# Attention scores of the first block from three float32r products instead of one float32 product, with the gate rows spilled to make room

## What is computed

```python
q = (rms_norm(c_q, q_norm) @ w_q_up).reshape(b, s, 8, 96)        # rank 256 -> 8 x 96
kv = (rms_norm(c_kv, kv_norm) @ w_kv_up).reshape(b, s, 8, 128)   # rank 128 -> keys 64, values 64
q = concat([q_nope, apply_rope(q_rope)]); k = concat([k_nope, apply_rope(k_rope)])
scores = einsum("bqhd,bkhd->bhqk", q, k) * 96 ** -0.5
mask = key_chunk <= q_chunk                                       # chunks of 64 tokens
probs = softmax(where(mask, scores, -inf)); o = probs @ v
```

## Time and profile before

| | us |
|---|---|
| median of 3 runs (2779.86 to 2781.82) | 2780.64 |
| the profiled execution, its own time | 2778.42 |
| its span in the profile | 2776.6 |
| attention of the first block, from the first maximum to the last values' products | 282 to 467 |
| delta rule after it | from 467 |

### The profile page before, as it was taken

One profiled execution on the slowest core, in us unless ns is written; L12 is line 12 of the kernel. 1 busy time (PEld: TensorE's weight loads), 2 busy tenths in 40 slices (PEclk: granted clock), 3 DMA queues, 4 the chain that ended last, 5 costly groups with the idle time before them and its releaser, 6 DMA issues.

```text
span 2776.6 us, 39285 instructions
## 1 busy us (share of the span) xinstructions
PE 2643.3 (95%) x15530; PEld 2137.2 (77%) x15530; DVE 1879.3 (68%) x2265; ACT 1237.7 (45%) x2316; POOL 408.6 (15%) x354
## 2 busy tenths in 40 slices
PE   7999998999799999999999999899998999999997
PEld 6887566887688888888778888655677888888886
DVE  3466554664687777888974664489646655578889
ACT  3323565332777773333553333467316433343332
POOL 4322001347300000000300000001375000000002
PEclk9999999999999999999999999999999999999999
DMA  3210000004356664332323123411253232343333
GB/s 135 54 38 15 8 6 25 3 21 171 106 168 211 189 198 164 117 121 107 137 91 121 62 91 106 168 60 35 89 196 112 101 111 103 122 164 109 121 106 122
DMA packets 213489, 290.49 MB, mean 105 GB/s; under 512 B 16552, under 2 KB 143807, under 8 KB 213311
## 3 DMA queue, kind: packets, MB, share of 16 engines
q1 hardware_dynamic: 195918, 227.75, 24.8%
q10 hardware_dynamic: 17392, 60.30, 5.5%
HBM read 220.91 MB, written 67.11 MB: 104 GB/s over the span
## 4 chain that ended last, share of the span: by engine, by line
PE 78%; DVE 11%; ACT 4%; POOL 3%; issue 3%; DMA 1%; SPq 0%; ACTq 0%; DVEq 0%; POOLq 0%
PE ps L1739 7%; PE ps L1741 7%; PE ps L1740 7%; PE ps L1794 6%; PE ps L1796 6%; PE ps L1795 6%; PE ps L1877 4%; PE ps L1879 4%; PE ps L1878 4%; PE ps L1530 3%; PE ps L1436 2%; PE ps L1309 1%; PE ps L1311 1%; PE ps L1310 1%; PE ps L1676 1%
## 5 line engine op out<-in xcount | busy, mean ns | idle before, releaser
L1794 PE MATMUL ps<-down_t_hi,down_s_hi 128*128 128x512 f32 x896 | 349.4, 390 | 4.0 <-DVE acc L3332 2.2
L1796 PE MATMUL ps<-down_t_hi,down_s_lo 128*128 128x512 f32 x896 | 348.7, 389 | 0.0
L1795 PE MATMUL ps<-down_t_lo,down_s_hi 128*128 128x512 f32 x896 | 348.6, 389 | 0.0
L2492 ACT CAST down_s_hi<-down_a 128x2048 fp32r<-128x2048 f32 x56 | 107.2, 1915 | 368.7 <-PE ps L1796 327.1
L1142 POOL TENSOR_SCALAR mean_sq<-ssq 128x1 f32<-128x1 f32 x64 | 36.6, 571 | 1294.7 <-ACT squares_junk_ffn L2030 1244.6
L1739 PE MATMUL ps<-act_hi,up_hi 128*128 128x512 f32 (+1 forms) x544 | 205.7, 378 | 6.1 <-issue 2.8
L1740 PE MATMUL ps<-act_lo,up_hi 128*128 128x512 f32 (+1 forms) x544 | 204.9, 377 | 0.0
L1741 PE MATMUL ps<-act_hi,up_lo 128*128 128x512 f32 (+1 forms) x544 | 204.8, 376 | 0.0
L1794 PEld LDWEIGHTS ps<-down_t_hi,down_s_hi 128*128 128x128 f32 x896 | 168.2, 188 | 41.7 <-issue 7.4
L1796 PEld LDWEIGHTS ps<-down_t_hi,down_s_lo 128*128 128x128 f32 x896 | 168.2, 188 | 35.3
L1795 PEld LDWEIGHTS ps<-down_t_lo,down_s_hi 128*128 128x128 f32 x896 | 168.2, 188 | 34.6
(11 more groups left out here) (383 smaller groups left out, 6511.6 us busy)
## 6 DMA issues: line engine op xcount, KB each, us to landing
down_a<-hid_spill SPq DMA_DIRECT2D x32, 1024.0 KB, 6.6
hid_spill<-up_hid ACTq DMA_DIRECT2D x30, 1024.0 KB, 6.2
w_ada<-in_w_ada SPq DMA_DIRECT2D x48, 512.0 KB, 4.0
up_raw<-in_w_in SPq DMA_DIRECT2D x18, 1024.0 KB, 5.1
raw<-in_w_out SPq DMA_DIRECT2D x32, 512.0 KB, 3.7
up_raw<-in_w_up SPq DMA_DIRECT2D x16, 1024.0 KB, 5.6
down_b<-in_w_down SPq DMA_DIRECT2D x16, 1024.0 KB, 6.5
up_raw<-in_w_mlp_in SPq DMA_DIRECT2D x16, 1024.0 KB, 5.3
```

The costliest lines, as they stand in the source:

```text
L1794: pe.matmul(out, ops["s_hi"][:, k, cols], ops["t_hi"][:, k, :], start=first, stop=False, skip_group_check=True)
L1795: pe.matmul(out, ops["s_hi"][:, k, cols], ops["t_lo"][:, k, :], start=False, stop=False, skip_group_check=True)
L1796: mm = pe.matmul(out, ops["s_lo"][:, k, cols], ops["t_hi"][:, k, :], start=False, stop=last, skip_group_check=True)
```

## The change

- The query and key tiles become two sets each, `q_hi`, `k_hi`, `q_lo`, `k_lo`. A score product becomes three float32r products. A width under 256 columns is made 256.
- High parts are written by ACT (`mla_take` into the hi tiles; `mla_rope_high` for the rotated rows), low parts by DVE from PSUM (`mla_low_part`) and from `rope_t` (`mla_rope_low`). Rotation sums go into `rope_t` instead of the query tile.
- The low tiles lie where the gate rows lay: SP stores the gate rows to memory (`gate_out`, eight transfers of 256 KB) after the panel loads, and brings them back (`gate_back`) when the last pair's scores have begun. `key_rotation` waits for the store, `gdn_out` for the return.
- For the first pair the projections come in the order 0, 2, 4, 1, 3, 5 (first halves first). `mla_rotate(0, 1)`, the last panel's silu, the low part of chunk 5 and the scales move from before the attention into steps 0, 1, 2, 3 and 10 of the first pair on DVE. PE's projections of the next pair wait for DVE's low parts where they waited for ACT's copies.
- The out-norm multiply of the gate rows moves behind all eight gated products.

```diff
+MLA_FIRST = (0, 2, 4, 1, 3, 5)
+MLA_FIRST_BANKS = (7, 1, 0, 3, 2, 6)
+MLA_FIRST_FEATS = (2, 5, 2, 5, 3, 6)
...
+        q_lo = [[sb(f"q_feat_lo{x}{h}", kb, [P, SEQ], F32R) for h, kb in enumerate(kbs)] for x, kbs in enumerate(((169, 173), (65, 69)))]
+        k_lo = [[sb(f"k_feat_lo{x}{h}", kb, [P, SEQ], F32R) for h, kb in enumerate(kbs)] for x, kbs in enumerate(((177, 181), (49, 53)))]
...
+            for t in range(NT):
+                sp.wait_ge(sem("gate_silu"), NT + t + 1)
+                sp.dma_start(gate_d[t], gate[:, t, :]).then_inc(sem("gate_out"), 16)
...
+            sp.wait_ge(sem("mla_scores"), SB_ITEMS * (MLA_PAIRS - 1))
+            for t in range(NT):
+                sp.dma_start(gate[:, t, :], gate_d[t]).then_inc(sem("gate_back"), 16)
...
-                if i and n in (2, 3):
-                    pe.wait_ge(sem("proj_read"), 8 * i + 2 * n - 1)
+                if i == 1 and n == 0:
+                    pe.wait_ge(sem("mla_feat_done"), MLA_FEAT_AT[0, "low", 1])
+                elif i == 1 and n == 1:
+                    pe.wait_ge(sem("mla_feat_done"), MLA_FEAT_AT[0, "sum", 1])
+                elif i and n in (2, 3):
+                    pe.wait_ge(sem("mla_feat_done"), MLA_FEAT_AT[i, "low", n - 2])
...
-                    pe.wait_ge(sem("proj_read"), 8 * i + 7)
+                    pe.wait_ge(sem("mla_feat_done"), MLA_FEAT_AT[i, "low", 4])
...
-                    w = min(HALF, n - f * HALF)
-                    mm = pe.matmul(ps[:, 2 * h + f, 0:w], q_f[i % 2][h][0:DQK, t * P:(t + 1) * P],
-                                   k_f[i % 2][h][0:DQK, f * HALF:f * HALF + w], start=True, stop=True)
+                    w = max(min(HALF, n - f * HALF), 2 * P)
+                    q, k = slice(t * P, (t + 1) * P), slice(f * HALF, f * HALF + w)
+                    pe.matmul(ps[:, 2 * h + f, 0:w], q_hi[i % 2][h][0:DQK, q], k_hi[i % 2][h][0:DQK, k], start=True, stop=False)
+                    pe.matmul(ps[:, 2 * h + f, 0:w], q_hi[i % 2][h][0:DQK, q], k_lo[i % 2][h][0:DQK, k], start=False, stop=False)
+                    mm = pe.matmul(ps[:, 2 * h + f, 0:w], q_lo[i % 2][h][0:DQK, q], k_hi[i % 2][h][0:DQK, k], start=False, stop=True)
...
             def mla_pair(i):   # ACT
...
+                    if i == 0 and s == 2:
+                        mla_rope_high(0, 1)
+                    if s in (5, 7) and not last:
+                        mla_rope_high(i + 1, s // 2 - 2)
+                    if i == 0 and s == 10:
+                        mla_key_copy(0, k_hi, k_hi[0][0])
+                        mla_key_copy(1, k_hi, k_hi[0][0])
+                    if i == 0 and s == 12:
+                        mla_key_copy(0, k_lo, k_lo[0][0])
+                        mla_key_copy(1, k_lo, k_lo[0][0])
...
+            def mla_low_part(i, n):   # DVE
+                cols = slice(n % 2 * HALF, (n % 2 + 1) * HALF)
+                hi, lo = (q_hi, q_lo) if n < 2 else (k_hi, k_lo)
+                dve.wait_ge(sem("proj_read"), mla_took(i, n))
+                for h in range(2):
+                    ins = dve.tensor_tensor(lo[i % 2][h][0:NOPE, cols], ps[h * NOPE:(h + 1) * NOPE, MLA_BANKS[n] if i else MLA_FIRST_BANKS[n], :],
+                                            hi[i % 2][h][0:NOPE, cols].bitcast(F32), ALU.subtract)
...
             def mla_pair(i):   # DVE
...
-                    if i == 0 and s == 5:
-                        dve.wait_ge(sem("v_prod"), NT)
-                        dve.tensor_copy(k_f[1][1][rr, :], k_f[0][0][rr, :]).then_inc(sem("mla_k_rope_done"), 1)
+                    if i == 0 and s == 0:
+                        mla_rotate(0, 1)
+                    if i == 0 and s == 1:
+                        conv_silu(GDN_PANELS - 1)
+                    if i == 0 and s == 2:
+                        mla_low_part(0, 5)
+                    if i == 0 and s == 3:
+                        mla_rope_low(0, 1)
+                    if i == 0 and s == 10:
+                        gdn_scales()
...
-                    if s - 1 in MLA_STEPS[2:4] and not last:
-                        mla_rotate(i + 1, MLA_STEPS.index(s - 1) - 2)
+                    if s in (2, 3) and not last:
+                        mla_low_part(i + 1, s - 2)
+                    if s == 4 and not last:
+                        mla_rotate(i + 1, 0)
+                    if s == 5 and not last:
+                        mla_rope_low(i + 1, 0)
+                    if s == 6 and not last:
+                        mla_rotate(i + 1, 1)
+                        mla_low_part(i + 1, 4)
+                    if s == 7 and not last:
+                        mla_rope_low(i + 1, 1)
+                    if s == 9 and not last:
+                        mla_low_part(i + 1, 5)
+
+            mla_rotate(0, 0)
+            mla_low_part(0, 0)
+            mla_low_part(0, 4)
+            key_low()
+            mla_rope_low(0, 0)
+            mla_low_part(0, 1)
             mla_max(0, 0)
```

More of the change, by code:

```diff
@@ L1492, in mla_pair @@
                         mla_sums(i, 0)
-            for n in range(MLA_CHUNKS):
+            for n in MLA_FIRST:
                 pe.wait_ge(sem("lat_feat_done"), MLA_FIRST_FEATS[n])
@@ L1500, in _ @@
             for t, b in enumerate(V_BANKS):
-                name, count = (("mla_k_rope_done", 1), ("mla_k_rope_done", 1), ("proj_read", 3), ("proj_read", 5),
-                               ("mla_rope_done", 1), ("mla_rope_done", 2), ("proj_read", 7), ("proj_read", 9))[t]
+                name, count = (("mla_k_rope_done", 1), ("mla_k_rope_done", 1), ("mla_feat_done", MLA_FEAT_AT[0, "low", 0]),
+                               ("mla_feat_done", MLA_FEAT_AT[0, "sum", 0]), ("mla_feat_done", MLA_FEAT_AT[0, "low", 4]),
+                               ("v_done", 1), ("v_done", 2), ("v_done", 3))[t]
                 pe.wait_ge(sem(name), count)
@@ L2106, in _, with mla_rope_high, mla_key_high, mla_key_copy @@
                 .then_inc(sem("g_exp_done"), 1)
+            rr = slice(NOPE, DQK)
+            def mla_rope_high(i, n):
+                cols = slice(n * HALF, (n + 1) * HALF)
+                act.wait_ge(sem("mla_feat_done"), MLA_FEAT_AT[i, "sum", n])
+                for h in range(2):
+                    act.copy(q_hi[i % 2][h][rr, cols], rope_t[rr, h * HALF:(h + 1) * HALF]).then_inc(sem("rope_hi"), 1)
+            def mla_key_high():
+                act.wait_ge(sem("mla_k_rope_done"), 1)
+                for h in range(2):
+                    act.copy(k_hi[0][h][rr, :], k_sum[rr, :]).then_inc(sem("rope_hi"), 1)
+            def mla_key_copy(h, dst, src):
+                act.copy(dst[1][h][rr, :], src[rr, :].bitcast(F32)).then_inc(sem("rope_hi"), 1)
+            def mla_take(i, n):
+                cols = slice(n % 2 * HALF, (n % 2 + 1) * HALF)
+                act.wait_ge(sem("mla_proj"), mla_chunk_count(i, n))
+                for h in range(2):
+                    act.copy((q_hi if n < 2 else k_hi)[i % 2][h][0:NOPE, cols],
+                             ps[h * NOPE:(h + 1) * NOPE, MLA_BANKS[n] if i else MLA_FIRST_BANKS[n], :]).then_inc(sem("proj_read"), 1)
             def conv_panel(i, j):
@@ L2201, in mla_pair @@
                         mla_out(i, 0)
[L2203 to L2204 removed]
+            mla_take(0, 4)
+            mla_key_high()
+            mla_take(0, 1)
+            mla_rope_high(0, 0)
+            mla_take(0, 5)
             for t, b in enumerate(V_BANKS):
@@ new lines, in mla_rope_low @@
+            def mla_rope_low(i, n):
+                cols = slice(n * HALF, (n + 1) * HALF)
+                dve.wait_ge(sem("rope_hi"), FROM["rope_hi"] + mla_rope_hi(i, n))
+                for h in range(2):
+                    ins = dve.tensor_tensor(q_lo[i % 2][h][rr, cols], rope_t[rr, h * HALF:(h + 1) * HALF],
+                                            q_hi[i % 2][h][rr, cols].bitcast(F32), ALU.subtract)
+                ins.then_inc(sem("mla_feat_done"), 1)
+                dve.wait_ge(sem("mla_feat_done"), MLA_FEAT_AT[i, "rope_low", n])
```

137 lines of the change are left out of this document (79 added, 58 removed).

## The result

| | before | changed |
|---|---|---|
| median of five runs, us | 2780.64 (2779.29 to 2781.93) | 2795.67 (2793.36 to 2796.73) |
| ratio to the kernel before, 95% interval | | 1.0052 (1.0037 to 1.0067) |
| profiled execution: own time, span, us | 2778.4, 2776.6 | 2793.4, 2791.6 |
| mean granted clock | 0.985 | 0.984 |

The changed kernel is 15.0 us slower, twice what was forecast (+7.7 us by the sum, named as 2788.0); it lies inside the range 2775 to 2798 and in the direction with the largest chance, but just outside the +2 to +14 that the prediction called the forecast's own range.

What follows compares the result with a forecast made beforehand. PE was taken as nearly full in the first block's attention, with DVE close to the path in pairs' first halves. Terms +6.5 + 3.2 - 2.0 = +7.7 us on 2778.4 gave 2786.1, named 2788 as median; range 2775 to 2798.

Steps and rivals of the forecast that it cites:

- pair 3: Last pair of the first block's attention: prepares no next pair, gets only PE's saving of 2.3, counted as -2.0 us.
- The scores on PE: Score products in the attention: three float32r products instead of float32 save 9.3 us of PE time, 2.3 in each pair.
- Ahead of pair 0: Stretch before the first pair: DVE work leaves and low parts come, so maximum 0 is 0.6 us earlier.
- Pair 0: First pair of the attention: DVE becomes the bound in steps 0 to 9; +6.5 us, bounds +3 to +10.
- the walk itself: Queue-by-queue timing of pair 0's first steps, putting maximum 10 at 312.3 instead of 305.1, 7.2 us later.
- Pairs 1 and 2: Middle pairs: PE waits some 3 us for low part 4; +1.6 us each, bounds for one -2 to +4.
- Rival (b): PE's new holes in pairs 0 to 2 lower its clock, adding 3 to 5 us: 2792; chance 20%.
- (a): DVE's additions in steps 2 to 9 of pairs 0 to 2 are hidden, PE's saving passes: 2771; chance 10%.
- (c): The sides cancel: pair 0 costs 4 us, pairs 1 and 2 nothing, +2 in all: 2782.6; chance 18%.
- (d): Three score products cost what two float32 records cost, so PE saves nothing: +14.7 us, 2795; chance 2%.
- At nothing: Gate rows' store and way back, and their multiplies moved behind eight products, outside the attention's path: no cost.
- What would show it: Expected trace signs: DVE without holes in pair 0, maximum 10 later by 7 and 3 us, score waits some 55.

Runs made afterwards that it cites:

- e3: Changed kernel with one float32 score product on the high tiles instead of three float32r products, low parts still made but left out of the result: 2803.4 us.
- e5: e1 with the second rotation of pairs 1 to 3 put back to its old step, after the maximum of step 6: 2778.4 us.
- e2: Changed kernel with DVE's low part of chunk 4 before the second rotation instead of behind it: 2791.9 us.
- e4: Changed kernel with spare products, results overwritten, keeping PE busy while it waits for DVE's low parts: 2789.0 us.
- e6: Changed kernel with pair 0's second rotation, two low parts, last panel's silu and block scales put back ahead of the first maximum: 2802.2 us.
- e10: Kernel before with only the gate rows' spill, return and second-pass multiply added: 2780.9 us, ratio 1.0001.
- e1: Changed kernel with DVE's low parts one column wide and all three score products reading the high tiles: 2778.9 us.
- e11: e9 with the rotated rows projected first for pairs 1 to 3: 2772.7 us, 0.9970 of the kernel before.
- e9: Changed kernel's three products for pairs 1 to 3 with high and low parts made on GpSimd, pair 0 as in the kernel before: 2782.1 us.
- e12: Kernel before, float32 scores and nothing spilled, with the rotated rows projected first: 2778.6 us.

## Why the prediction was right, and by how much it was off

The direction, the place and the mechanism of DVE's queue were right; the size was half of what was measured, and a second mechanism, the clock, was left out of the sum. DVE's additions to the first halves cost more than PE's cheaper scores give back; pair 0 is worst; pair 3 gains; the rest of the program is untouched. Point by point:

- **The scores on PE, -9.3 in all.** The term is too large. In the second halves of pairs 1 and 2 the saving was 0.94 us (16.98 to 16.04), not 1.4; pair 3 gave -1.7, not -2.0, and four times that is 6.7. e3's 7.7 holds some clock too. Start to start, the first float32r product behind a turn takes 0.31 to 0.32 us (303.15 to 303.46) where the earlier trace rows gave 0.23 between products in a row. (The 0.47 in the expectation of e5 is such a record's duration.)
- **Ahead of pair 0, 0.6 earlier.** It was 0.4 later, 1.0 off, inside the bounds named there (1 earlier to 2 later). This point moves with the clock ahead of it: e2, which has the changed kernel's work up to there, began pair 0 3.0 us earlier.
- **Pair 0, +6.5: the step that failed.** It measured +10.5, above its upper bound of +10. The forecast had maximum 10 at 312.3 and 0.7 less to the pair's end. It came at 316.0, and the end added 0.2 more. By e4, where PE does not wait at half clock there, maximum 10 is at 314.4. So 1.6 of the 3.7 us is clock; 1.0 is the later start; the other 1.1 is the walk itself, or the half clock behind the hole at 292.88, which e4 did not take away (0.91 from 282 to 300). The second half lost PE's saving: 17.2 us against 17.0, where 0.7 less was forecast. The trace has ACT's key copies ahead of what PE waits for there; e6 rules the scales out. That the key copies alone do it was not tested.
- **Pairs 1 and 2, +1.6 each.** They cost 3.2. In e4 they are 49.36 us, +1.65: the queue's part was sized right, with two errors that cancel (the first halves +2.6 instead of +3.0, the second -0.9 instead of -1.4). The other 1.5 us of each is the half clock behind the hole of 3.77 us, which the prediction foresaw as "some 3 us" but at full clock.
- **Rival (b), the clock, 20%.** It was put as an alternative to the forecast, with 2792. It came together with it, in all three pairs, at 4.7 us by rows and 6.7 by medians: its own 3 to 5 for what it took. The objection to it was that holes of up to 2 us had left the clock at 1.00. That was one execution: in e10 the same hole of 1.93 us halved the clock. Of the earlier trace rows, which the prediction calls on for a long idle gap of PE, only 470 to 480 has idle time; from 220 to 230 the clock fell with PE busy for 10.00 of 10 us. With PE kept busy the kernel is at 2789.0 by its median, beside the forecast's 2788 (by its trace, whose last maximum is at 465.3, it is still 11.0 us above the kernel before, against 7.7). This is the error of method: a rival that follows from the forecast's own holes should have been a term of its sum.
- **Rivals (a), (c), (d).** (a) would need the additions hidden; e1 says they and their effects are 16.8 us. (c) fell with pair 0's +10.5 and the +3.2 of pairs 1 and 2. (d) named 2795, the number nearest to what was measured, and it is refuted by e3, by pair 3's -1.7 and by the products 0.23 apart: there the number would have been right by luck.
- **At nothing.** e10 has the spill, its way back and the multiplies in a second pass at 1.0001. That moving work into pair 0 gives back 4.4 to 6.5 us (e6) was not foreseen as a gain; the prediction had costed this part as 6.9 us more of work in pair 0 against 0.6 earlier ahead of it, without asking what the old place would cost once low parts are added.
- **What would show it.** As named: no hole of DVE between maxima 1 and 10 of pair 0 (the largest is 0.51 us up to maximum 8; then 1.71 and 1.99 for PE at half clock), three records 0.23 apart, a hole ahead of each last projection. Maximum 10 came 10.7 us later in pair 0, not 7, and 4.1 in pair 1 counted from its start, not 3. Waits for scores fell to 63, not to 55.

What stays open: how the 1.1 us of pair 0's walk divide, why the medians give the half clock 6.7 us and the traces 4.7, and by which condition a hole of 1.9 us halves the clock or doesn't. Not tried was e11 with GpSimd's key rows made after pair 0's rotations.

## What to carry to other kernels

A cheaper product needs its operands made, and the price is paid by whoever makes them, at the moment when others queue behind: here some 7 us less of PE brought DVE's low parts on the path, which cost 17 us with the clock behind them, while an idle engine could do the same work (e9) and leave the time as it was. Once a bound has moved, a hole of TensorE can have a second price behind it, its clock, 1.5 us for each of these; count it in the sum, not beside it. And a saving on the bound engine passes only as far as its waits allow: 0.7 us of 2.3 with the rotations beside GpSimd's work, 2.1 once they were moved.

## What the runs showed of the hardware that was not expected

Beside GpSimd's operations, one form of DVE's operations keeps its length and another one doubles. In e11 GpSimd makes a high and a low part of key rows while DVE works on a rotation; the two timelines:

```profile
285.23 1.04 POOL L1244 TENSOR_SCALAR k_feat_hi<-k_feat 32x1024 fp32r<-32x1024 f32 x1
286.35 2.33 POOL L1247 TENSOR_TENSOR k_feat_lo<-k_feat,k_feat_hi 32x1024 fp32r<-32x1024 f32 x1
```

```profile
285.63 0.69 DVE L2957 TENSOR_TENSOR rope_tmp<-ps,rope_trig 64x512 f32<-64x512 f32 x1
286.33 0.68 DVE L2958 TENSOR_TENSOR rope_tmp<-ps,rope_trig 64x512 f32<-64x512 f32 x1
287.05 2.88 DVE L2961 TENSOR_TENSOR q_feat<-rope_tmp 32x512 f32<-32x512 f32 x2
...
292.22 1.38 DVE L2961 TENSOR_TENSOR q_feat<-rope_tmp 32x512 f32<-32x512 f32 x2
```

DVE's products with one operand in PSUM take their usual 0.69 and 0.68 us beside GpSimd, the first one begun while GpSimd's operation ran. The sums, whose operands both lie in SBUF, take 2.88 instead of 1.38: they end 1.25 us after GpSimd's operation does, at 289.93 against 288.68. The Trainium skill (SBUF — State Buffer, on the two separate sides of SBUF) has a rule for this: DVE operations with two SBUF inputs and GpSimd's share a pair of ports, and whoever comes second is blocked until the other's instruction ends. The trace agrees: 1.63 us of overlap (287.05 to 288.68) cost 1.50. The long sums of e9 (346.82 to 349.33) fit it too: GpSimd's low part of another feature ends at 348.78 there. In e11 PE stood 2.20 us for that rotation and then ran at half clock (0.91 from 282 to 300); pair 0 of e11 is 2.2 us longer than that of e12.

The clock's fall behind equal holes (1.93 us, e10 against the kernel before) was the other surprise: 1.00 and 0.94 in the stretch 300 to 330 for the same instructions.
